# A two-layer hybrid decoder on eight cores: reads tracked apart, diagonals and pooled sums on GpSimd, activations time-major

## The chip, the cores and the metric

One Trainium2 chip, 8 NeuronCores. Every core works on two of the sixteen sequences with the same program; no core talks to another. The metric is the device time of the slowest core in microseconds. In the profile TensorE is PE (its weight loads PEld), VectorE DVE, ScalarE ACT, GpSimd POOL, SyncE SP.

## What is computed

The reference, cut to what the change touches:

```python
# x: (16, 2048, 1024); per layer (2 layers), h = rms_norm(x) @ w_in, split in za, zb, zc
a, gate = split(za); y = a * sigmoid(gate)              # mixer A: 384 channels
y = causal_depthwise_conv(y, width 31) + conv_b
ya = silu(layer_norm(y)) @ w_pw
u, v = split(gelu(zb)); v = layer_norm(v)               # mixer B: 4 heads x 96
yb = u * (tril(w_s) @ v per chunk of 128 + b_s)
yc = ((trailing mean over 2/4/8/16 positions of zc) - zc) @ w_pool * pool_scale   # mixer C
x = x + concat(ya, yb, yc) @ w_out
x = x + (silu(rms_norm(x) @ w_gate) * (rms_norm(x) @ w_up)) @ w_down
# after the last layer: rms_norm(x)
```

## The kernel before

The residual `xT` stays in SBUF in float32, channels on partitions, 2048 positions, in four tiles j of 512. A layer runs so: for each tile norm1 makes `xb` (bf16, not yet divided by the rms) and the factor `r1`; `A` (L626) makes the gated values of the tile, `ytok`, stores them to DRAM (`yd`) and reads them back in another order, `y2`, by eight DMAs of 16 partitions each (L648 on). `toep_closures` (L653) spreads the filter taps into `toep`. `conv` (L667) multiplies `y2` (as the stationary operand) with `toep` and leaves `xc`, 128 blocks on partitions, 384 channels x 16 positions in a block free. `lna_closures` (L682) and `lnt` (L707) do the LayerNorm over channels, per position of the block, and transpose into `silT` with SiLU. `V` (L719) and `U` (L744) project mixer B's halves with Gelu, V's LayerNorm gives `vn`; `SP` (L754) mixes positions, `TR` (L763) transposes. `Zprep` (L774) makes r along the free axis: `split` writes r in three bf16 parts, `dia` multiplies an identity by them into twelve diagonals `dsp`, `bc` multiplies those by ones on TensorE. `Z` (L779) projects mixer C, scales by that broadcast `rbc` into `zc`, and builds the trailing sums by doubling; `PM` (L806) applies `w_pool`. `PW` (L812), `WO` (L821), `norm2` (L833; it uses the same diagonals) and the `FFN` follow. Between two sequences `fin_store` (L598) transposes the result and stores it by way of `osA` (three buffers) and `osB` (two), from the same SyncE queue that carries `yd` and `y2`.

What sets the order: every engine executes its own queue in program order. `P.add` (L89) puts the instruction at the end of its engine's queue and computes its semaphore waits from `Buf` objects: a writer waits for the last writer and all readers of the same `Buf`, and of every `Buf` whose byte range overlaps (`ov`, L80 to L83). A DMA's completion is a semaphore too, so a DMA that writes a `Buf` waits, on the queue that issues it, until the DMA that wrote the `Buf` before has landed. Small work is put into the queues between matmul groups: `push` (L384) appends a closure to `bg` (or to `lo`), each `tick` (L393) executes the first of `bg`, or of `lo` where `bg` is empty, `need(tag)` (L400) executes `bg` until the tag is done, `drain` (L408) executes all. PSUM has eight banks, given out in turn; a matmul waits for the bank's last reader.

`w_a`, `w_uv` come by two DMAs each into one `Buf`; `load_w_rest` (L441) ends with the triangular mask of `wsT`, a GpSimd operation that waits for that DMA. All constants, identity included, share one `Buf`, `bC`. Weights are loaded by GpSimd's queue. The order by hand in the main loop before, tile by tile: V0, U0, conv, Zprep0, SP0, V1, Z0, Zprep1, TR0, U1, PM0, SP1, V2, Z1, ... Z3, TR3, `lnt` 1 to 3, then PW and WO.

## Time and profile before

| what | us |
|---|---|
| median of 3 runs (lowest to highest) | 3668.67 (3633.67 to 3855.72) |
| profiled execution, whole | 3630.46 |
| its span, slowest core (cores 3613.8 to 3628.2) | 3628.2 |
| PE busy / DVE / ACT / POOL over the span | 2787.5 / 1384.3 / 820.5 / 276.7 |
| mean granted TensorE clock (1 is 2.4 GHz, 0.5 is 1.2 GHz) | 0.886 |
| a half of `w_a` or `w_uv` from issue to landing, median | 10.1 / 10.7 |
| one read `y2` from issue to landing, median (48 KB, 512 packets) | 2.2 |
| a store `yd` from issue to landing, median | 2.8 |

The span is what the stages below are cut from; 2.3 us of the execution lie around it. Pieces of the mixer, from the grouped view, mean of one in ns: sum with PSUM `zc` 683, `xc` from PSUM 692, `ybt` 617 (four a tile), `bn_stats` of `vg` 560 and of `xc` 784, each with an aggregate of 182, apply on `xc` 639, pow on GpSimd 1013 to 1024, `pp` 975, the five small ones of `split` 165 each (about 1.35 us with their gaps). A projection of 16 matmuls of 512 columns took 3.62 us at full clock, V's 32 matmuls of 384 columns 5.4 us.

Times are us from the start of the span. In a timeline a row has start, length, engine, line, operation, what it writes and reads, how many are merged, and in brackets the engine's idle time just before and what ended it. A line is mostly that of a helper (L365 `tt`, L371 `ts`, L377 `stt`, L355 `act_op`, L326 `mm`, L318 `dma`), so one goes by the names of tiles.

### The profile page before, as it was taken

The numbers are of one execution on the slowest core, as the hardware profiler recorded it, in microseconds if no ns is written. First come the engines' busy times: TensorE is split into PE (matmuls) and PEld (weight loads), VectorE is DVE, ScalarE is ACT, GpSimd is POOL, SyncE is SP. The second block draws the span as 40 slices with busy tenths as digits, with TensorE's granted clock in tenths as the row PEclk, the third lists the DMA queues.
The fourth block names the chain that finished last, engine by engine and source line by source line (L and its number), as shares of the span: only waits on it lengthen the run. The fifth ranks groups of instructions, "written<-read, shape, count | busy, mean of one in ns | idle before, by whom it ended". The sixth has DMA issues, their size and how long they took to land.

```text
span 3628.2 us, 43607 instructions; the slowest of 8 cores (3613.8 to 3628.2 us)
## 1 busy us (share of the span) xinstructions
PE 2787.5 (77%) x14864; PEld 1387.4 (38%) x14864; DVE 1384.3 (38%) x2657; ACT 820.5 (23%) x1240; POOL 276.7 (8%) x347
## 2 busy tenths in 40 slices
PE   4444879999824679999955448899997346799998
PEld 3332334444422334444443223344444223344444
DVE  2264433323435352233433535233232453432335
ACT  3314210011512421100333242100124124101102
POOL 1012000000011101000000220100000121000000
PEclk9776989999966789999987768899998677899999
DMA  7301232120210305221332030412102003012212
GB/s 152 53 1 20 39 58 53 24 41 12 42 25 1 58 1 81 41 41 30 100 110 43 1 58 2 75 35 41 24 12 50 17 1 58 12 25 52 36 23 93
DMA packets 123847, 148.98 MB, mean 41 GB/s; under 512 B 71664, under 2 KB 98800, under 8 KB 121584
## 3 DMA queue, kind: packets, MB, share of 16 engines
q0 software_dynamic: 36224, 96.61, 15.9%
q1 hardware_dynamic: 87408, 49.59, 4.9%
q8 instruction: 124, 2.03, 0.2%
q14 instruction: 91, 0.75, 0.1%
HBM read 219.71 MB, written 23.07 MB: 67 GB/s over the span
## 4 chain that ended last, share of the span: by engine, by line
PE 65%; DMA 12%; DVE 11%; issue 5%; POOL 4%; ACT 2%; DVEq 1%; SPq 0%; POOLq 0%; ACTq 0%
PE bank L326 62%; DMA y<-yd 8%; DVE dsp L371 3%; DMA yd<-ytok 2%; POOL zF L365 2%; ACT silT L355 1%; PE bank L336 1%; PE bank L344 1%; POOL zG L365 1%; DVE h2T L377 1%; DVE ybt L377 1%; DVE pp L377 1%; DVE vg L377 1%; DVE bnv L730 1%; DMA w_a_sb<-w_a 1%
## 5 line engine op out<-in xcount | busy, mean ns | idle before, releaser
L326 PE MATMUL bank<-h2T,ring 128*128 128x512 bf16 x5632 | 1237.3, 383 | 39.4 <-DVE h2T L377 39.4
L326 PEld LDWEIGHTS bank<-h2T,ring 128*128 128x128 bf16 x5632 | 553.8, 99 | 718.4 <-issue 67.1
L326 PE MATMUL bank<-act,wd 128*128 128x512 bf16 x2816 | 618.1, 379 | 7.5 <-DVE r L371 3.7
L365 DVE TENSOR_TENSOR xT<-xT,bank 128x512 f32<-128x512 f32 x640 | 439.8, 687 | 473.1 <-PE bank L326 394.8
L365 DVE TENSOR_TENSOR act<-tsil,bank 128x512 bf16<-128x512 f32 x352 | 242.0, 688 | 973.7 <-PE bank L326 961.9
L355 ACT ACTIVATE tsil<-bank 128x512 f32<-128x512 f32 x352 | 210.1, 597 | 1588.6 <-PE bank L326 1585.5
L326 PEld LDWEIGHTS bank<-act,wd 128*128 128x128 bf16 x2816 | 269.9, 98 | 323.4 <-issue 8.0
L326 PE MATMUL bank<-dsp,onesb 128*128 128x512 bf16 x96 | 41.1, 558 | 355.3 <-DVE dsp L371 355.3
L355 ACT ACTIVATE sqr<-xT 128x512 bf16<-128x512 f32 x320 | 192.5, 623 | 205.1 <-PE bank L524 194.0
L336 PE MATMUL bank<-toep,y 128*128 128x128 bf16 x576 | 45.0, 253 | 196.1 <-DMA y<-yd 196.1
L326 PE MATMUL bank<-w_uv_sb,xb 128*128 128x384 bf16 x1024 | 193.3, 351 | 0.0
L326 PE MATMUL bank<-w_a_sb,xb 128*128 128x384 bf16 x1024 | 178.8, 331 | 1.7 <-DVE r L371 1.7
L326 PEld LDWEIGHTS bank<-dsp,onesb 128*128 128x128 bf16 x96 | 8.6, 113 | 374.4 <-issue 373.4
L326 PEld LDWEIGHTS bank<-w_uv_sb,xb 128*128 128x128 bf16 x1024 | 107.1, 105 | 83.3 <-issue 27.8
L326 PEld LDWEIGHTS bank<-w_a_sb,xb 128*128 128x128 bf16 x1024 | 97.0, 99 | 63.1 <-issue 6.5
L336 PEld LDWEIGHTS bank<-toep,y 128*128 128x128 bf16 x576 | 44.6, 157 | 197.5 <-issue 197.5
L371 DVE TENSOR_SCALAR dsp<-identb,spb 128x128 bf16<-128x128 bf16 x384 | 97.4, 254 | 42.2 <-DVE dsp L371 3.0
L326 PE MATMUL bank<-ya,wo 128*128 128x512 bf16 x384 | 112.9, 406 | 0.0
L326 PE MATMUL bank<-ybT,wo 128*128 128x512 bf16 x384 | 108.6, 393 | 0.0
L355 ACT ACTIVATE silT<-bank,pv 128x512 bf16<-128x512 f32 x48 | 107.6, 2655 | 0.1
L318 POOL DMA_DIRECT2D ring<-w_gate_up x88 | 47.1, 539 | 739.9 <-PE bank L326 715.2
L344 PE MATMUL bank<-identF,xc 128*128 128x128 f32 x192 | 35.7, 351 | 83.4 <-DVE xc L372 80.6
(100 smaller groups left out, 1893.4 us busy)
## 6 DMA issues: line engine op xcount, KB each, us to landing
ring<-w_gate_up POOLq DMA_DIRECT2D x88, 512.0 KB, 7.3
wd<-w_down POOLq DMA_DIRECT2D x12, 1536.0 KB, 11.7
xst<-x SPq DMA_DIRECT2D x32, 512.0 KB, 10.1
out<-osF SPq DMA_DIRECT2D x16, 512.0 KB, 5.0
w_a_sb<-w_a POOLq DMA_DIRECT2D x8, 768.0 KB, 10.1
w_uv_sb<-w_uv POOLq DMA_DIRECT2D x8, 768.0 KB, 10.7
yd<-ytok SPq DMA_DIRECT2D x16, 384.0 KB, 2.8
y<-yd SPq DMA_DIRECT2D x128, 48.0 KB, 2.2
```

Source lines behind the costliest of these rows:

```text
L318: return P.add(q, lambda e, out=out, in_=in_: e.dma_start(out=out, in_=in_), reads=reads, writes=writes, dma=True, final=final)
L326: ins = e.matmul(out, l, r, start=(first and i == 0), stop=(last and i == n - 1))
L336: ins = e.matmul(out, l, r, start=(i == 0), stop=(i == n - 1))
L344: ins = e.transpose(out, in_, idn)
L355: return e.activation(out=out, in_=in_, func=func, **kw)
L365: return P.add(eng, lambda e, out=out, in0=in0, in1=in1, op=op: e.tensor_tensor(out=out, in0=in0, in1=in1, op=op), reads=reads, writes=writes)
L371: return e.tensor_scalar(out=out, in0=in0, scalar1=s1, scalar2=None, op0=op0)
L377: e.scalar_tensor_tensor(out=out, in0=in0, scalar=scalar, in1=in1, op0=op0, op1=op1),
L730: vec(lambda e, q=q: e.bn_stats(out=bnv[:, q * 6:q * 6 + 6], in_=vg[:, q, :]), [vg.b(q, lo=1536 * q, n=1536)], [bst])
```

## The change

`Buf` gets a group: ranges of the same group don't count as overlapping. With it each of the eight reads into `y2`, and each half of `w_a` and `w_uv`, is tracked on its own. The twelve diagonal writes on VectorE become one GpSimd `tensor_tensor` of 128x1536 with both inputs broadcast. In Z both chains of sums are issued on GpSimd, the ScalarE copies of the lower partitions go (tile halves are written directly, or copied on GpSimd), and what reads them on VectorE (`fin`) is queued behind four empty closures each. `silT` is stored time-major, so that ScalarE writes in order; PW reads it with a stride and writes PSUM in order. V's LayerNorm becomes closures; `vn` and `pp` get a second buffer. The constants come before the first weight load and have two `Buf`s, the mask comes after A(3). The order of the main loop is new. The diff, cut to its core (not shown: the buffers' places, `vconv` and `toep` with `bC2`, `w_a.b(0 or 1)` in A's read lists):

```diff
-    def buf(self, *key, rng=None):
+    def buf(self, *key, rng=None, grp=None):
...
                 for o in self.ranged:
+                    if grp is not None and o.grp == grp:
+                        continue
                     if o.rng[0] < rng[1] and rng[0] < o.rng[1]:
...
-        dma("gpsimd", w_a[:, :, DA:2 * DA], w_a_d[l, :, :, DA:2 * DA], [], [w_a.b()])
-        dma("gpsimd", w_a[:, :, 0:DA], w_a_d[l, :, :, 0:DA], [], [w_a.b()])
+        dma("gpsimd", w_a[:, :, DA:2 * DA], w_a_d[l, :, :, DA:2 * DA], [], [w_a.b(1, grp="w_a")])
+        dma("gpsimd", w_a[:, :, 0:DA], w_a_d[l, :, :, 0:DA], [], [w_a.b(0, grp="w_a")])
...
         dma("gpsimd", wsT[:], w_s_d[l], [], [B("wsT")])
+
+    def mask_ws():
         pool(lambda e: e.affine_select(out=wsT[:], in_=wsT[:], pattern=[[0, 4], [1, 128]], compare_op=ALU.is_ge,
                                        fill=0.0, base=0, channel_multiplier=-1), [B("wsT"), bC], [B("wsT")])
...
     x_dma(0, 0)
-    load_w_a(0)
     pool(lambda e: e.memset(identF[:], 1.0), [], [bC])
...
     pool(lambda e: e.memset(ocS[:], 1.0 / 1024.0), [], [bC])
+    load_w_a(0)
+    dma("sync", pv[:], pv_d, [], [bPV])
     x_dma(0, 1)
     x_dma(0, 2)
-    dma("sync", pv[:], pv_d, [], [bPV])
...
-        def dia(i):
-            for q in range(4):
-                ts(dsp[:, i, q, :], identb[:], spb[:, i, q:q + 1], None, ALU.mult, None, [bs, bC], [bd])
+        def dia():
+            tt(dsp[:].rearrange("p i q t -> p (i q) t"), identb[:].unsqueeze(1).to_broadcast([128, 12, 128]),
+               spb[:].rearrange("p i q -> p (i q)").unsqueeze(2).to_broadcast([128, 12, 128]), ALU.mult,
+               [bs, bC], [bd], eng="gpsimd")
...
         push(split)
-        push(lambda: dia(0))
-
-        def dia12():
-            dia(1)
-            dia(2)
-        push(dia12)
+        push(dia)
+        if late is not None:
+            late()
         push(bc, (kind + "bc", s, l, j))
...
-    def y2b(u):
+    def y2b(u, i):
         if u < 0:
             return y2.b("h", n=2 * 2 * NG)
-        return y2.b(u, lo=(2 + 32 * u) * NG * 2, n=32 * NG * 2)
+        return y2.b(u, i, lo=(2 + 32 * u) * NG * 2, n=32 * NG * 2, grp="y2")
...
             dma("sync", y2[TB * i:TB * (i + 1), 2 + 32 * j:2 + 32 * (j + 1), :], src[i, :, 32 * j:32 * (j + 1), :],
-                [byd], [y2b(j)])
+                [byd], [y2b(j, i)])
...
-            mms(groups, [y2b(u) for u in range(-1, NJ)] + [toep_b(b)], [bb])
+            mms(groups, [y2b(-1, 0)] + [y2b(u, i) for u in range(NJ) for i in range(NI)] + [toep_b(b)], [bb])
...
-            dst = silT[:, ct, :].rearrange("p (b t) -> p t b", t=TB)[:, 4 * tq:4 * tq + 4, :]
+            dst = silT[:, ct, 4 * tq:4 * tq + 4, :]
             act_op(dst, bk[:].rearrange("p (t b) -> p t b", t=4), AF.Silu, [bb, bPV],
-                   [silT.b(ct, tq, lo=4096 * ct, n=4096)], scale=pvc(l, PV_LNG + ct), bias=pvc(l, PV_LNB + ct))
+                   [silT.b(ct, tq, lo=4096 * ct + 1024 * tq, n=1024)], scale=pvc(l, PV_LNG + ct), bias=pvc(l, PV_LNB + ct))
...
     def V(s, l, j):
-        rd = [bxb(j, k) for k in range(8)] + [w_uv.b()]
+        def vstat(q):
+            bst = B("bnv")
+            vec(lambda e: e.bn_stats(out=bnv[:, q * 6:q * 6 + 6], in_=vg[:, q, :]),
+                [vg.b(q, lo=1536 * q, n=1536)], [bst])
+            vec(lambda e: e.bn_aggr(out=bnv[:, 24 + 2 * q:26 + 2 * q], in_=bnv[:, q * 6:q * 6 + 6]), [bst], [bst])
...
             tick()
+            push(lambda q=q: vstat(q))
+            tick()
         bst = B("bnv")
-        for q in range(4):
-            vec(lambda e, q=q: e.bn_stats(out=bnv[:, q * 6:q * 6 + 6], in_=vg[:, q, :]),
-                [vg.b(q, lo=1536 * q, n=1536)], [bst])
-        for q in range(4):
-            vec(lambda e, q=q: e.bn_aggr(out=bnv[:, 24 + 2 * q:26 + 2 * q], in_=bnv[:, q * 6:q * 6 + 6]), [bst], [bst])
-        mvv = bnv[:, 24:32].rearrange("p (q t) -> p q t", t=2)
-        ts(bnv[:, 32:36], mvv[:, :, 1], LN_EPS, None, ALU.add, None, [bst], [bst])
-        pool(lambda e: e.tensor_tensor(out=bnv[:, 32:36], in0=bnv[:, 32:36], in1=mhalf[:, 0:4], op=ALU.pow),
-             [bst, bC], [bst])
-        for q in range(4):
+        vn = vn2[j % 2]
+
+        def pw():
+            mvv = bnv[:, 24:32].rearrange("p (q t) -> p q t", t=2)
+            ts(bnv[:, 32:36], mvv[:, :, 1], LN_EPS, None, ALU.add, None, [bst], [bst])
+            pool(lambda e: e.tensor_tensor(out=bnv[:, 32:36], in0=bnv[:, 32:36], in1=mhalf[:, 0:4], op=ALU.pow),
+                 [bst, bC], [bst])
+
+        def ap1(q):
             stt(vg[:, q, :], vg[:, q, :], bnv[:, 24 + 2 * q:25 + 2 * q], sgB[:, 0, :], ALU.subtract, ALU.mult,
                 [vg.b(q, lo=1536 * q, n=1536), bst, sgB.b()], [vg.b(q, lo=1536 * q, n=1536)])
+
+        def ap2(q):
             stt(vn[:, q, :], vg[:, q, :], bnv[:, 32 + q:33 + q], sgB[:, 1, :], ALU.mult, ALU.add,
                 [vg.b(q, lo=1536 * q, n=1536), bst, sgB.b()], [vn.b(q, lo=768 * q, n=768)])
+        push(pw)
+        for q in range(4):
+            push(lambda q=q: ap1(q))
+        for q in range(4):
+            push(lambda q=q: ap2(q), ("vn", s, l, j) if q == 3 else None)
...
-            tick()
+            tick(2)
 
     def SP(s, l, j):
+        need(("vn", s, l, j))
+        vn = vn2[j % 2]
         for h in range(4):
...
-            tick()
...
+    def Zprep(s, l, j, late=None):
         def sink(bk, bb):
             act_op(rbc[:], bk[:], AF.Copy, [bb], [rbc.b()])
-        split_bcast_closures(s, l, j, r1, "r1", sink)
+        split_bcast_closures(s, l, j, r1, "r1", sink, late)
...
             tt(zc[:, m, ZH:ZH + NT], bk[:], rbc[:], ALU.mult, [bb, rbc.b()], [zc.b()])
-            tick()
+            tick(2)
         W = ZH + NT
+        z0, z1 = zc[:, 0, :], zc[:, 1, :]
+
+        def pt(out, i0, i1, rd, wr):
+            tt(out, i0, i1, ALU.add, rd, wr, eng="gpsimd")
+
+        def m0():
+            pt(zG[:, 1:W], z0[:, 1:W], z0[:, 0:W - 1], [zc.b()], [zG.b()])
+            pt(zF0[64:128, :], zG[64:128, ZH:W], zG[64:128, ZH - 2:W - 2], [zG.b()], [zF0.b()])
+            pt(zF0[0:64, :], z0[0:64, ZH:W], z0[0:64, ZH - 1:W - 1], [zc.b()], [zF0.b()])
+
+        def m1():
+            pt(zG[:, 1:W], z1[:, 1:W], z1[:, 0:W - 1], [zc.b(), zF0.b()], [zG.b()])
+            pt(zF[:, 3:W], zG[:, 3:W], zG[:, 1:W - 2], [zG.b()], [zF.b()])
+            pt(zG[:, 7:W], zF[:, 7:W], zF[:, 3:W - 4], [zF.b()], [zG.b()])
+            pt(zF[64:128, ZH:W], zG[64:128, ZH:W], zG[64:128, ZH - 8:W - 8], [zG.b()], [zF.b()])
+            pool(lambda e: e.tensor_copy(out=zF[0:64, ZH:W], in_=zG[0:64, ZH:W]), [zG.b()], [zF.b()])
+
+        def fin(m):
+            f = zF0[:, :] if m == 0 else zF[:, ZH:W]
+            fb = zF0.b() if m == 0 else zF.b()
+            zm = zc[:, m, :]
+            out, ob = (pp0, B("pp0")) if m == 0 else (pp1, pp1.b())
+            stt(out[:], f, invw[:, m:m + 1], zm[:, ZH:W], ALU.mult, ALU.subtract, [fb, zc.b(), bC2], [ob])
+            if j == 0:
+                tt(f[:, 0:ZH], f[:, 0:ZH], invcnt[:, m, :], ALU.mult, [fb, bC2], [fb])
+                tt(out[:, 0:ZH], f[:, 0:ZH], zm[:, ZH:2 * ZH], ALU.subtract, [fb, zc.b()], [ob])
+        m0()
+        m1()
+        for i in range(4):
+            push(lambda: None)
+        push(lambda: fin(0))
+        for i in range(4):
+            push(lambda: None)
+        push(lambda: fin(1), ("pp", s, l, j))
+
+    def PM(s, l, j):
+        need(("pp", s, l, j))
         for m in range(2):
-            zm = zc[:, m, :]
-            tt(zG[:, 1:W], zm[:, 1:W], zm[:, 0:W - 1], ALU.add, [zc.b()], [zG.b()], eng="gpsimd")
-            tt(zF[:, 3:W], zG[:, 3:W], zG[:, 1:W - 2], ALU.add, [zG.b()], [zF.b()], eng="gpsimd")
-            if m == 1:
-                tt(zG[:, 7:W], zF[:, 7:W], zF[:, 3:W - 4], ALU.add, [zF.b()], [zG.b()], eng="gpsimd")
-                tt(zF[:, 15:W], zG[:, 15:W], zG[:, 7:W - 8], ALU.add, [zG.b()], [zF.b()], eng="gpsimd")
-            act_op(zF[0:64, ZH:W], zG[0:64, ZH:W], AF.Copy, [zG.b()], [zF.b()])
-            stt(pp[:, m, :], zF[:, ZH:W], invw[:, m:m + 1], zm[:, ZH:W], ALU.mult, ALU.subtract,
-                [zF.b(), zc.b(), bC], [pp.b()])
-            if j == 0:
-                tt(zF[:, ZH:2 * ZH], zF[:, ZH:2 * ZH], invcnt[:, m, :], ALU.mult, [zF.b(), bC], [zF.b()])
-                tt(pp[:, m, 0:ZH], zF[:, ZH:2 * ZH], zm[:, ZH:2 * ZH], ALU.subtract, [zF.b(), zc.b()], [pp.b()])
-
-    def PM(s, l, j):
-        for m in range(2):
-            bk, bb = next_bank()
-            mm(bk[:], [(wpl[:, m, :], pp[:, m, :])], [pp.b(), B("wpl")], [bb])
+            bk, bb = next_bank()
+            mm(bk[:], [(wpl[:, m, :], (pp0 if m == 0 else pp1)[:])], [B("pp0") if m == 0 else pp1.b(), B("wpl")], [bb])
             act_op(yc[j][:, m, :], bk[:], AF.Identity, [bb, bPV], [yc[j].b()], scale=pvc(l, PV_PS + m))
 
     def PW(s, l, j):
         y = ya[j % 2]
         for co in range(3):
             bk, bb = next_bank()
-            mm(bk[:], [(w_pw[:, ci, co * 128:(co + 1) * 128], silT[:, ci, jc(j)]) for ci in range(3)],
-               [silT.b(ci, tq, lo=4096 * ci, n=4096) for ci in range(3) for tq in range(4)] + [B("w_pw")], [bb])
+            mm(bk[:].rearrange("p (b t) -> p b t", t=TB),
+               [(w_pw[:, ci, co * 128:(co + 1) * 128],
+                 silT[:, ci, :, 32 * j:32 * (j + 1)].rearrange("p t b -> p b t")) for ci in range(3)],
+               [silT.b(ci, tq, lo=4096 * ci + 1024 * tq, n=1024) for ci in range(3) for tq in range(4)] + [B("w_pw")], [bb])
...
             drain()
+            mask_ws()
+            V(s, l, 0)
+            U(s, l, 0)
             load_wo(l, 0)
             load_wo(l, 1)
-            V(s, l, 0)
-            U(s, l, 0)
-            conv()
+
+            def cv():
+                while bg:
+                    pop(bg)
+                conv()
+            Zprep(s, l, 0, cv)
             lna_closures(s, l)
-            Zprep(s, l, 0)
-            SP(s, l, 0)
-            V(s, l, 1)
-            Z(s, l, 0)
-            Zprep(s, l, 1)
-            TR(s, l, 0)
-            U(s, l, 1)
-            PM(s, l, 0)
-            SP(s, l, 1)
...
-            PM(s, l, 2)
-            SP(s, l, 3)
-            lnt(s, l, 0)
-            Z(s, l, 3)
-            load_wo(l, 2)
-            TR(s, l, 3)
-            lnt(s, l, 1)
-            lnt(s, l, 2)
-            lnt(s, l, 3)
+            for j in range(NJ):
+                Z(s, l, j)
+                if j + 1 < NJ:
+                    Zprep(s, l, j + 1)
+                    need(("vn", s, l, j))
+                    V(s, l, j + 1)
+                SP(s, l, j)
+                TR(s, l, j)
+                if j + 1 < NJ:
+                    U(s, l, j + 1)
+                else:
+                    for tq in range(4):
+                        lnt(s, l, tq)
+                    load_wo(l, 2)
+                PM(s, l, j)
             for fp in range(NRING):
                 load_ring(l, fp, fp)
             PW(s, l, 0)
-            PM(s, l, 3)
             load_wd(l, 0)
             PW(s, l, 1)
```

## Rows read from the trace of the kernel before

**Rows 1.** Waits over the span: engine line, waited for, us in total, times, longest.

```profile
PE bank L326 <- DVE dsp L371: 355.3, 32, 23.0
...
PE bank L336 <- DMA y<-yd: 196.1, 4, 56.4
...
PE bank L344 <- DVE xc L372: 80.6, 8, 15.3
...
PE bank L344 <- DVE osB L377: 35.9, 2, 18.2
```

**Rows 2.** Timeline of SyncE's DMA queue, and a window: busy by engine, PEclk, DMA share, GB/s.

```profile
1021.36 0.38 SPq L318 DMA_DIRECT2D yd<-ytok  x1
...
1026.32 16.64 SPq L318 DMA_DIRECT2D y<-yd  x8
...
1000.00:1016.00 16.00, 0.00 (x0) 0.00 (x0) 0.00 (x0) 0.00 (x0) 0.00 (x0) 0.50 0.17 21
```

**Rows 3.** Timeline before conv, second layer, TensorE and ScalarE.

```profile
978.27 10.56 PE L326 MATMUL bank<-w_uv_sb,xb 128*128 128x384 bf16 x64
...
990.03 0.93 ACT L355 ACTIVATE toep<-vconv,M 128x768 bf16<-128x768 bf16 x1 [0.62 <-DVE toep L371]
...
1045.27 11.06 PE L336 MATMUL bank<-toep,y 128*128 128x128 bf16 x144 [56.43 <-DMA y<-yd]
```

**Rows 4.** Windows behind it: conv to zc of tile 0, three cycles, LayerNorm tail.

```profile
1045.27:1078.07 32.80, 26.12 (x227) 18.78 (x227) 24.36 (x55) 2.92 (x5) 1.08 (x2) 0.89 0.01 1
...
1078.07:1195.88 117.81, 51.61 (x279) 28.34 (x279) 59.92 (x149) 33.24 (x48) 25.95 (x23) 0.71 0.00 1
...
1195.88:1227.31 31.43, 5.59 (x24) 4.88 (x25) 9.92 (x19) 22.71 (x13) 11.53 (x14) 0.50 0.29 47
```

**Rows 5.** Timeline of one tile cycle, GpSimd, VectorE and TensorE.

```profile
1120.10 1.06 POOL L365 TENSOR_TENSOR zG<-zc 128x527 f32<-128x527 f32 x1 [7.18 <-DVE zc L365]
...
1123.30 1.57 POOL L365 TENSOR_TENSOR zG<-zc 128x527 f32<-128x527 f32 x1 [0.93 <-ACT zF L355]
...
1127.47 1.26 POOL L365 TENSOR_TENSOR zF<-zG 128x513 f32<-128x513 f32 x1
...
1129.63 0.75 DVE L377 SCALAR_TENSOR_TENSOR pp<-zF,invw,zc 128x512 bf16<-128x512 f32 x1 [5.68 <-ACT zF L355]
...
1131.85 4.23 DVE L371 TENSOR_SCALAR dsp<-identb,spb 128x128 bf16<-128x128 bf16 x12
...
1136.33 1.44 PE L326 MATMUL bank<-dsp,onesb 128*128 128x512 bf16 x3 [22.10 <-DVE dsp L371]
```

**Rows 6.** Grouped by form: xcount, busy us, mean ns, then idle before.

```profile
L377 DVE SCALAR_TENSOR_TENSOR vn<-vg,bnv,sgB 128x384 bf16<-128x384 f32 x64 | 39.5, 618 | 6.7
...
L730 DVE BATCH_NORM_STATS2 bnv<-vg 128x6 f32<-128x384 f32 x64 | 35.9, 560 | 129.4 <-ACT vg L355 124.4
...
L448 POOL TENSOR_SCALAR_AFFINE_SELECT wsT<-wsT 128x512 bf16<-128x512 bf16 x4 | 2.5, 634 | 51.1 <-DMA wsT<-w_s 51.1
```

**Rows 7.** Grouped by form: ScalarE's SiLU outputs, TensorE's weight loads.

```profile
L355 ACT ACTIVATE silT<-bank,pv 128x512 bf16<-128x512 f32 x48 | 107.6, 2655 | 0.1
...
L355 ACT ACTIVATE tsil<-bank 128x512 f32<-128x512 f32 x352 | 210.1, 597 | 1588.6 <-PE bank L326 1585.5 <-DVE h2T L377 3.2
...
L336 PEld LDWEIGHTS bank<-toep,y 128*128 128x128 bf16 x576 | 44.6, 157 | 197.5 <-issue 197.5
...
L326 PEld LDWEIGHTS bank<-silT,w_pw_sb 128*128 128x128 bf16 x144 | 15.1, 107 | 57.6 <-issue 44.7
```

**Rows 8.** Timeline of the start, GpSimd and TensorE.

```profile
26.51 0.88 POOL L318 DMA_DIRECT2D w_a_sb<-w_a  x1 [23.87 <-DMA w_a_sb<-w_a]
...
33.58 0.66 PE L344 MATMUL bank<-identF,xst 128*128 128x128 f32 x2 [33.58 <-DVE invcnt L498]
...
65.30 0.63 POOL L448 TENSOR_SCALAR_AFFINE_SELECT wsT<-wsT 128x512 bf16<-128x512 bf16 x1 [19.75 <-DMA wsT<-w_s]
...
66.45 1.07 POOL L538 TENSOR_TENSOR r<-r,mhalf 128x4 f32<-128x4 f32 x1
```

71 lines of the change are left out of this document (33 added, 38 removed).

## The prediction, made before the kernel was run

> **What bounds the kernel now.** I read the profile in this order: the sum of waits over the whole run, the stages of one layer, then that layer's queues in order of time. No engine is the bound over the run. In the waits [rows 1] the reader is to see four pauses of TensorE that all lie inside the token mixer: 355.3 us for `dsp` (the diagonals that broadcast r), 196.1 us for the reshuffled `y2`, 80.6 us for the normalised `xc`, 35.9 us for `osB`. Together 668 us of 3628. The FFN, where TensorE is dense, isn't touched by the change. So I work out the mixer of the second layer and carry it to all four (two sequences, two layers).
>
> First, the convolution's input. SyncE sends the eight reads of a tile one behind another: 16.64 us for eight [rows 2], because all eight write one `Buf` (`y2b(j)`), and each waits until the one before has landed, though they fill other partitions. While that goes on the DMA engines are 0.17 busy [rows 2]. TensorE ends U(0) at 978.27 + 10.56 = 988.8, and starts conv at 1045.27, 56.4 later [rows 3]; the mean over four layers is 196.1/4 = 49.0 [rows 1]. Second, the stages behind it [rows 4]: conv to the second `zc` of tile 0 32.8 us, three tile cycles 117.8 (39.3 each, granted clock 0.71), the LayerNorm tail up to PW(0) 31.4. VectorE is busy 59.9 of the 117.8, so it is order and latency, not load, that sets a cycle. Rows 5 show how: GpSimd builds the pooled sums from 1120.10 to 1128.7, with a trip to ScalarE in each half; VectorE stands in its queue at `pp` until 1129.63, and `split` and the twelve `dsp` writes (4.23 us) are behind it, so that TensorE, which had all else done, waits 22.10 us.
>
> **The change, part by part** (second layer, then times four).
>
> *Reads tracked apart.* In the new order the last `yd` store leaves at about 979.4, right after the last `ytok`. From its issue to the first read that waits for it took 1026.32 less 1021.36, 5 us, in a busy moment [rows 2]; I take 4. Eight reads are issued in about 3 us (the issue of a DMA on SyncE took 0.3 to 0.4), and the last lands about 2.2 later: near 989. DMA capacity: 0.17 of sixteen engines for 16 us is 2.7 us of all sixteen, which fits. The next thing that is late is ScalarE: its last `toep` ends at 990.03 + 0.93 = 991.0 [rows 3], then come a table load of 1.3 and the first Gelu, which frees the first PSUM bank at about 993. So 56.4 becomes about 4, and over the run 196.1 - 4 x 4 = 180 us go. Behind it VectorE has V(0)'s LayerNorm (four statistics, pow, eight applies: 3.8 + 1.7 + 5.0 from 992.8, with the split 1004.6) and then twelve conv evictions at 0.65, to 1012.4; rbc lies over `cbB`, so it waits for the last of them; second `zc` about 1016.5. From conv start 23.5 us against 32.8 [rows 4]: -9 a layer.
>
> *Tile cycle.* New path from one second `zc` to the next: eight GpSimd operations at a pitch of 1.2 for the long ones (1.06 and a hop, [rows 5]), 9.3; `fin(1)` 0.75 + 0.3; split 1.35; diagonals on GpSimd; broadcast 1.2 + 0.2; U's last three products 3.9 at 2.4 GHz or 6.5 in part at 1.2, 5.2 taken; PM 0.5; Z 3.6; `zc` 0.9. V (5.4 us) now lies beside the GpSimd chain, and the two ScalarE copies are gone. The diagonals aren't in the trace as a GpSimd operation. 128x527 took 1.06 us [rows 5], 2.0 ns an element, so 1536 elements are 3.1 us; bounds: the one-input 128x512 at 0.634 [rows 6], three times, 1.9; the slow 1.57 of the same sum [rows 5], scaled, 4.6. I take 3.1 + 0.2, because the form is the same. Sum 26.6, say 27, against 39.3: -37 a layer for three cycles. VectorE's load in such a cycle is about 16 us (eight applies at 0.62 [rows 6], statistics 3.5, `ybt` 2.8, the rest 4.5), so it doesn't become the bound; GpSimd has 9.3 + 3.3 + 1.0.
>
> The slow 1.57 started while VectorE's `pp` ran [rows 5], 0.5 more than its neighbours. By the Trainium skill, "SBUF — State Buffer", section "Who interferes with whom", a VectorE instruction with two SBUF inputs and a GpSimd instruction that reads SBUF exclude each other; by that rule the applies and `ybt` may each push the GpSimd chain or be pushed, and the trace agrees as far as this one row goes. It speaks against moving diagonals to GpSimd. The sum goes by the unslowed row; if every second GpSimd operation were slowed by 0.5 it would be 2.3 more a cycle, 27 us over the run.
>
> *LayerNorm work.* Ticks: a cycle has 24 slots (Z 4, V 8, TR 4, U 8), and its `bg` queue now gets 26 entries (eight empty, two `fin`, three of Zprep, four statistics, pw, eight applies), so `lo`, which holds conv's LayerNorm, is served only by the four ticks of Z(0). Nearly all of it falls behind Z(3): `ts` and pow wait behind the GpSimd chain (10.7 after `zc`), applies and `fin` to 13.9, then three groups of 3.9 statistics + 1.5 pow + 2.3 applies (and one 0.7), to 37.7, transposes 2.8, activation 0.6. Tail about 41.5 against 31.4 [rows 4]: +10 a layer. In that tail the SiLU output before cost 2655 ns each, its write being strided, where a like operation with a plain write costs 597 [rows 7]; the 2 us saved each are hidden now behind VectorE, except the last ones, which the 41.5 holds.
>
> *The price of time-major.* PW now reads its moving operand with 256 bytes between neighbours. 36 matmuls a layer. No moving read like it is in the trace. Lower bound zero: the matmul could hide it. Nearest row: TensorE's own strided read, `y2` as weights, 157 ns against 107 for `w_pw` [rows 7], about a doubling of the streaming part; the far one is the strided write of ScalarE, 2655/597 = 4.4 times. Taking a doubling, 0.22 on 512 columns: +8 a layer; at 4.4 times, 0.73 each, +26 a layer. By the Trainium skill, "SBUF — State Buffer", in the note on cachelines under "Door 1: The DMA port swizzle (why `[64,N]` ≈ `[32,N]`)", each access that crosses to a new 16-byte line pays a penalty. The trace agrees for weights and for ScalarE's writes; for the moving side no row here shows it.
>
> *Start.* GpSimd waits for the first half of `w_a` before it makes the constants (26.51), TensorE starts at 33.58, and `r` stands on GpSimd behind the `wsT` mask until 65.30 [rows 8]. Now the constants come first, halves don't wait for each other, the mask comes after A(3). The second half of `w_a` should land near 37 (26.5 plus the 10.1 that such a half takes, page, part 6), where TensorE now resumes at 68.9: -30, bounds -20 (it lands at 47) and -35.
>
> *Second sequence.* Its `osB` stores stand on SyncE behind eight reads. 35.9 us in two waits [rows 1]; store and landing remain, 4 each: -28.
>
> *Costed at nothing:* norm2's diagonals on GpSimd (3.3 against 4.23 on VectorE, [rows 5], four a layer). GpSimd's earlier ring and `wd` loads wait for the tail and PM(3), which end before. If they didn't, each such wait would show before a broadcast.
>
> Sum: four times (-45 - 9 - 37 + 10 + 8) = -292, -30, -28: -350. Against the profiled execution 3628 - 350 = 3278, with 2.3 us around the span 3280. The median of the runs is 38 above the profiled one, the lowest 3 above; I forecast 3290.
>
> **Rivals.**
> 1. *The strided read costs as much as the strided write.* +26 instead of +8 a layer: 3362. For: both kinds of strided access in the trace are slow. Against: TensorE's own is only 1.5 times.
> 2. *The cycle doesn't shorten.* The broadcast ends up behind GpSimd, whose queue takes pooled sums, pow and diagonals in turn, or the `fin` slots come too late: 39.3 stays, +148, 3438. Against: the slots before `fin(1)` are over when V and SP are.
> 3. *Parallel reads aren't parallel.* If eight still took 17 us, 180 and 28 stay: 3498. Against: 0.17 DMA share.
> 4. *Slower than before.* One mechanism: the 256-byte stride on the moving side. It has to eat 350 + 32 = 382 us over 144 matmuls, 2.65 each, so it decides from 3.0 us a matmul. ScalarE's strided write took 2.655 for 512 elements, which still leaves 3628 - 382 + 327 = 3573. Only beyond that is it slower, say 3650.
> 5. *More is gained*: moving read free, low clock gone: 3220.
>
> **How the numbers follow.** Forecast (3220 to 3345) 0.66; rival 1 0.13; rival 2 0.09; rival 3 0.03; rival 4 0.02; rival 5 (below 3220) 0.07. The range 3215 to 3390 takes the forecast and rival 1 whole and a little of 2 and 5: about 0.82. About 2% is what a measurement of this kernel tells from no change. Slower by over 2% 0.02, within 2% (3595 to 3742) 0.02, all else 0.96.
>
> **What would show it.** In the profile after: TensorE's wait for `y` under 10 us a layer, the eight reads issued within 3 us; `dsp` a GpSimd operation of about 3.1 us; distance between second `zc`s about 27; wait for `xc` grown to some 30 us a layer; `silT` near 0.6; the PW matmul at 0.6 rather than 0.38; TensorE's first transpose well before 30. Wrong would be: a PW matmul over 1 us, GpSimd late at every broadcast, or the reads still 2 us apart.

## The result and the profile after

Measured beside the kernel before: 0.932 of its time, 95% interval 0.921 to 0.943; profiled execution 3401.28 us (before 3630.46), median of 4 runs 3457.65 (3397.40 to 3720.51) against 3655.48 of the kernel before, run in turn with it. In two of the four executions a whole die ran slower, which lifts the median; the ratios here and below leave such executions out. Faster by 6.8% where 9.4% had been forecast (3290 of 3630), and outside the range on its slow side. Cores that do the same work ended 55 us apart, and pairs of them (0 and 1, 2 and 3, 6 and 7) had a lower granted clock, 0.81, for a while, the longest stretches lying in the FFN. So core 5, which had none of that, shows what the kernel does, and core 0, the last to end, sets the time.

The cores of after, span and mean granted clock:

```profile
core 0: 3399.7 us, clock 0.892
...
core 5: 3344.8 us, clock 0.914
```

The stages, cut by the same marks in every kernel; "zc 2" is the start of the second `zc` of a tile, "tail" below is the stretch from there in tile 3 to PW(0). Four values are the four passes (two sequences, two layers); before is its slowest core, 3628.2.

| stage | before | after, core 5 | sum of the four | forecast |
|---|---|---|---|---|
| V(0) begins for the first time | 121.6 | 88.8 | -33 | -30 |
| V(0) to conv | 57.4, 67.0, 47.4, 66.5 | 15.7, 17.3, 16.9, 17.3 | -171 | -180 |
| conv to zc 2 of tile 0 | 31.7, 32.1, 32.4, 32.2 | 20.7, 19.1, 19.6, 19.1 | -50 | -36 |
| three tile cycles, each | 39.18, 39.27, 38.67, 39.51 | 27.05, 26.45, 27.02, 26.46 | -149 | -148 |
| zc 2 of tile 3 to PW(0) | 32.2, 32.1, 32.1, 32.1 | 42.4, 42.3, 42.2, 42.3 | +41 | +40 |
| PW(0) to the first `down` product | 196.2, 196.3, 198.9, 196.1 | 222.4, 222.4, 222.5, 222.4 | +102 | +32 |
| first `down` product of pass 2 to V(0) of pass 3 (second sequence, A part) | 504.4 | 481.3 | -23 | -28 |

Together -283, the difference of the two spans. All rows but one came out within 14 us of their forecast. The rows that follow are of core 0, up to the strided product. The waits over the span (engine line, waited for, us in total, times, longest), to be held against [rows 1]:

```profile
PE bank L331 <- POOL dsp L370: 110.1, 28, 6.0
...
PE bank L349 <- DVE xc L377: 78.2, 16, 5.6
```

`dsp` waits fell from 355.3 to 110.1, but not all of these 245 us were won: TensorE now waits 59.5 us for `ybt` and 25.0 for `vn`, which the list of before doesn't have. `y` and its 196.1 are gone from the list, and the reads of the last tile are issued in 4.14 us where they took 16.64 [rows 2]. SyncE's DMA queue, last `yd` and the reads behind it:

```profile
921.47 0.38 SPq L323 DMA_DIRECT2D yd<-ytok  x1
926.81 4.14 SPq L323 DMA_DIRECT2D y<-yd  x8
```

One tile cycle of after, GpSimd and TensorE, for [rows 5]:

```profile
955.94 1.06 POOL L370 TENSOR_TENSOR zG<-zc 128x527 f32<-128x527 f32 x1 [8.65 <-DVE zc L370]
...
964.86 0.60 POOL L831 COPY zF<-zG 64x512 f32<-64x512 f32 x1
965.37 1.44 PE L349 MATMUL bank<-identb,ybt 128*128 128x128 bf16 x12 [7.00 <-DVE ybt L382]
968.23 2.75 POOL L370 TENSOR_TENSOR dsp<-identb,spb 128x1536 bf16<-128x1536 bf16 x1 [2.78 <-DVE spb L575]
...
971.23 1.18 PE L331 MATMUL bank<-dsp,onesb 128*128 128x512 bf16 x3 [2.42 <-POOL dsp L370]
```

The whole chain of sums stays on GpSimd, from 955.94 to 965.46; the diagonals are one operation of 2.75; TensorE waits 2.42 for them, not 22.10, and 7.00 for `ybt` ahead of that. The windows that answer to [rows 4] (conv to zc 2, three cycles, tail; cut, as there, at the end of the `zc`):

```profile
935.96:955.73 19.77, 18.88 (x184) 15.21 (x185) 16.50 (x36) 2.29 (x5) 4.91 (x5) 0.88 0.51 82
955.73:1036.63 80.90, 56.67 (x284) 28.80 (x281) 48.27 (x96) 23.62 (x41) 37.81 (x30) 0.81 0.00 1
1036.63:1078.15 41.52, 14.67 (x66) 11.72 (x67) 29.17 (x54) 12.15 (x16) 14.04 (x14) 0.59 0.08 13
```

The row that missed is the one with the strided product. By form, before and then after:

```profile
L326 PE MATMUL bank<-silT,w_pw_sb 128*128 128x512 bf16 x144 | 39.4, 426 | 35.8 <-ACT silT L355 35.8
...
L331 PE MATMUL bank<-silT,w_pw_sb 128*128 128x512 bf16 x144 | 125.7, 1036 | 1.7 <-ACT silT L360 1.7
...
L360 ACT ACTIVATE silT<-bank,pv 128x512 bf16<-128x512 f32 x48 | 36.3, 776 | 64.5 <-PE bank L349 63.1
```

Overlapping matmuls inflate the mean; merged runs give the pitch (a run also holds the drain of its last product, so 9 come out 0.01 to 0.02 us dearer each than 18). Second layer, core 5 of after: 18 in 15.63 us, then twice 9 in 7.89, 0.87 each. Before, 9 took 2.11 at full clock, 0.23 each; the first nine of its pass took 3.54, most of it at a granted 0.50. First before, then after:

```profile
1231.12 2.11 PE L326 MATMUL bank<-silT,w_pw_sb 128*128 128x512 bf16 x9
...
1050.81 15.63 PE L331 MATMUL bank<-silT,w_pw_sb 128*128 128x512 bf16 x18 [0.42 <-ACT silT L360]
...
1082.14 7.89 PE L331 MATMUL bank<-silT,w_pw_sb 128*128 128x512 bf16 x9
```

The `silT` output on ScalarE fell from 2655 ns [rows 7] to 776; those 90 us of ScalarE lay mostly behind VectorE in the new tail; e2 finds that they bought 4.7 us a pass.

### The profile page after: what moved, and what is told of

Same layout as the page of the kernel before. It is cut to its first block, busy times and chain, and to the rows that moved or that the text cites. A ratio compares the mean times of both kernels' runs of the same rounds, so it can differ in the third digit from the quotient of the medians.

```text
span 3399.7 us, 43152 instructions; the slowest of 8 cores (3344.8 to 3399.7 us)
## 1 busy us (share of the span) xinstructions
PE 2990.8 (88%) x14864; PEld 1428.0 (42%) x14864; DVE 1312.5 (39%) x2273; ACT 736.4 (22%) x1208; POOL 395.7 (12%) x411
## 4 chain that ended last, share of the span: by engine, by line
PE 78%; DVE 7%; POOL 7%; issue 3%; DMA 2%; ACT 2%; SPq 0%; DVEq 0%; POOLq 0%; ACTq 0%
PE bank L331 75%; POOL dsp L370 2%; POOL zF L370 2%; PE bank L349 1%; POOL zG L370 1%; DVE bna L696 1%; DVE xc L377 1%; DMA w_a_sb<-w_a 1%; DVE h2T L382 1%; PE bank L532 1%; ACT toep L360 1%; PE bank L341 1%; DVE vn L382 1%; DVE zc L370 0%; POOL bna L701 0%
## 5 line engine op out<-in xcount | busy, mean ns | idle before, releaser
L331 PE MATMUL bank<-h2T,ring 128*128 128x512 bf16 x5632 | 1269.6, 390 | 31.5 <-DVE h2T L382 31.5
L331 PE MATMUL bank<-act,wd 128*128 128x512 bf16 x2816 | 630.8, 384 | 7.5 <-DVE rF L376 3.7
L331 PE MATMUL bank<-w_uv_sb,xb 128*128 128x384 bf16 x1024 | 210.4, 372 | 0.0
L323 POOL DMA_DIRECT2D ring<-w_gate_up x88 | 46.9, 537 | 839.1 <-PE bank L331 838.7
L331 PE MATMUL bank<-dsp,onesb 128*128 128x512 bf16 x96 | 41.9, 568 | 110.1 <-POOL dsp L370 110.1
L546 POOL TENSOR_TENSOR r<-r,mhalf 128x4 f32<-128x4 f32 x32 | 32.6, 1020 | 859.4 <-DVE r L376 840.5
L331 PE MATMUL bank<-silT,w_pw_sb 128*128 128x512 bf16 x144 | 125.7, 1036 | 1.7 <-ACT silT L360 1.7
L331 PE MATMUL bank<-ya,wo 128*128 128x512 bf16 x384 | 124.3, 439 | 0.0
L331 PE MATMUL bank<-ybT,wo 128*128 128x512 bf16 x384 | 118.1, 421 | 0.0
L349 PE MATMUL bank<-identF,xc 128*128 128x128 f32 x192 | 44.7, 421 | 78.2 <-DVE xc L377 78.2
L532 PEld LDWEIGHTS bank<-ocS,sqr 128*128 128x128 bf16 x1280 | 70.3, 98 | 68.5 <-issue 30.8
L370 POOL TENSOR_TENSOR dsp<-identb,spb 128x1536 bf16<-128x1536 bf16 x32 | 87.9, 2748 | 77.2 <-DVE spb L575 64.6
L382 DVE SCALAR_TENSOR_TENSOR h2T<-xT,pv,bank 128x512 bf16<-128x512 f32 x128 | 88.2, 741 | 18.8 <-PE bank L331 18.8
```

Of the source, the lines that this page charges most:

```text
L323: return P.add(q, lambda e, out=out, in_=in_: e.dma_start(out=out, in_=in_), reads=reads, writes=writes, dma=True, final=final)
L331: ins = e.matmul(out, l, r, start=(first and i == 0), stop=(last and i == n - 1))
L349: ins = e.transpose(out, in_, idn)
L370: return P.add(eng, lambda e, out=out, in0=in0, in1=in1, op=op: e.tensor_tensor(out=out, in0=in0, in1=in1, op=op), reads=reads, writes=writes)
L382: e.scalar_tensor_tensor(out=out, in0=in0, scalar=scalar, in1=in1, op0=op0, op1=op1),
L532: ins = e.matmul(bk[:, q:q + 1], sqr[i][:, q * 128:(q + 1) * 128], ocS[:, 0:1], start=(k == 0 and q == 0), stop=(k == 7), skip_group_check ...
```

## The experiments

Four questions: is the 102 us the stride of the moving operand; what does a stride cost; how much of the forecast's sum belongs to the reads; and what are the 55 us between core 0 and core 5. Where a kernel has a core without the granted 0.81, called undisturbed here, the times are taken on it. e3, e4, e7, e10 and e13 were executed once each.

### e1: PW reads `silT` in order

```diff
-            mm(bk[:].rearrange("p (b t) -> p b t", t=TB),
+            mm(bk[:].rearrange("p (t b) -> p t b", t=TB),
                [(w_pw[:, ci, co * 128:(co + 1) * 128],
-                 silT[:, ci, :, 32 * j:32 * (j + 1)].rearrange("p t b -> p b t")) for ci in range(3)],
+                 silT[:, ci, :, 32 * j:32 * (j + 1)]) for ci in range(3)],
-            act_op(y[:, co, :], bk[:], AF.Copy, [bb], [y.b()])
+            act_op(y[:, co, :].rearrange("p (b t) -> p b t", t=TB), bk[:].rearrange("p (t b) -> p b t", t=TB), AF.Copy,
+                   [bb], [y.b()])
```

> The changed kernel with one thing different: PW reads silT in the order it lies in (runs of 32 neighbours, 64 bytes), its result stays time-major in PSUM, and ScalarE's copy into ya reorders it while reading PSUM. Theory A (the missing time is the 256-byte stride of PW's moving operand): 18 PW matmuls took 15.63 us, 0.87 each, against 2.11 for 9 (0.23 each) in the kernel before, so 36 x 0.64 = 23 us a layer go, and with them the low granted clock behind PW (3 us a layer): about 100 us of the whole, 3400 becomes 3300 on the slowest core. Theory B (the WO part is longer because the denser mixer draws the clock down, and the PW matmuls merely stretch with it): the matmuls stay over 0.5 us, and the stretch from PW(0) to the FFN stays over 145 us. Theory C (the granted 0.81 in the first 120 us of the FFN comes from the slow PW matmuls ahead of it): the FFN stretch of the first sequence goes from 440 back to 419 on all cores; if it comes from the dense mixer, 0.81 stays.

Measured: 3325.03 profiled, median 3314.85 (before, run in turn with it, 3635.14), where 3300 was expected. PW(0) to the first `down` product is 191.9 us on core 3 in its first pass, against 222.4; in the other passes, and on core 1 in all four, about 211.6. The matmul is back at a mean of 379 ns, so theory A's price of the stride holds and B falls. The reordering moved into ScalarE's read of PSUM and costs nothing there: `ya` 595 ns, 597 in after, where it was plain. Grouped by form, core 1:

```profile
L331 PE MATMUL bank<-silT,w_pw_sb 128*128 128x512 bf16 x144 | 33.0, 379 | 1.7 <-ACT silT L360 1.7
L360 ACT ACTIVATE ya<-bank 128x512 bf16<-128x512 f32 x48 | 28.2, 595 | 122.5 <-PE bank L331 120.0 <-ACT ya L360 0.4
```

The 20 us that come back in those passes are a clock, not work. Core 1, windows in the FFN (us, PE, PEld, DVE, ACT, POOL busy, granted clock, DMA share, GB/s):

```profile
380.00:390.00 10.00, 5.33 (x13) 1.95 (x14) 4.53 (x7) 0.60 (x1) 0.00 (x0) 0.50 0.01 2
390.00:400.00 10.00, 10.00 (x39) 4.13 (x38) 1.75 (x3) 1.20 (x2) 4.75 (x7) 0.81 0.53 77
...
530.00:540.00 10.00, 10.00 (x48) 4.54 (x47) 2.06 (x3) 1.77 (x3) 1.06 (x2) 1.00 0.54 81
```

After half-busy work at 0.50 TensorE is granted 0.81, where core 3 was granted 1.00 in its first pass: 39 products in 10 us, later 48. 0.50 and 1.00 are its two levels, 1.2 and 2.4 GHz; 0.81 is neither, and shows also in windows of 5 us. So the stride is one cause, and the 0.81 a second one. It is there without the slow products, so they aren't what brings it about (theory C). Whether the shorter mixer does was the question for running the same kernel again.

### e12: the same kernel again, at another time and on another chip

No edit against e1.

> e1 once more, word for word. In e1, e2 and the changed kernel most cores took 45 to 105 us more than the least disturbed one, in pairs of cores, with a granted clock of 0.81 at the head of the first two FFNs; e3, e4, e6, e8, e9 and the kernel before hardly show it. Theory D (it belongs to this order of work): the profile shows 0.81 stretches again, and more than half of the core executions are 45 us and more above the lowest. Rival E (it was the chip's state at that hour): it is gone, all cores at about 3225.

Measured: 3235.32 profiled, ratio 0.889 (0.887 to 0.891). All cores end between 3223.4 and 3233.7, PW(0) to `down` is 191.8 to 193.1 everywhere, and no core shows 0.81. Core 5 where e1 had its 0.81:

```profile
390.00:400.00 10.00, 10.00 (x48) 4.56 (x47) 2.07 (x3) 1.79 (x3) 5.56 (x8) 1.00 1.01 134
400.00:500.00 100.00, 100.00 (x465) 45.30 (x463) 33.58 (x49) 10.15 (x17) 2.64 (x5) 1.00 0.53 75
```

The same instructions with and without it: the kernel alone doesn't set off the 0.81. It isn't the chip alone either: e6, e8 and e9 below ran later on the chip of e1 and have none in their profiled executions. But the kernel may still matter, alone or together with the chip and the hour: of the profiled executions after has it on six cores, e1 on eight, e2 on six, e3 and e7 on two each, while before, e4 and the seven others have it on none. So what sets it off stays open. Without it the 30.5 us a pass can be laid out. Windows from PW(0) on, second layer, core 5 of after, then core 5 of this kernel:

```profile
1050.81:1066.50 15.69, 15.69 (x19) 2.31 (x20) 0.00 (x0) 4.11 (x7) 3.29 (x7) 0.58 1.00 181
1066.50:1140.00 73.50, 64.11 (x262) 23.00 (x261) 21.98 (x42) 14.41 (x25) 7.54 (x4) 0.83 0.17 26
1140.00:1195.00 55.00, 47.37 (x242) 20.72 (x240) 22.08 (x38) 11.41 (x20) 3.76 (x2) 0.89 0.00 1
```

```profile
1023.48:1027.50 4.02, 4.02 (x19) 1.84 (x20) 0.00 (x0) 3.65 (x7) 3.29 (x7) 1.00 0.80 103
1027.50:1082.00 54.50, 47.56 (x262) 21.20 (x259) 21.81 (x42) 14.42 (x26) 4.97 (x4) 0.94 0.52 80
1082.00:1137.00 55.00, 44.84 (x242) 20.28 (x242) 22.18 (x39) 11.22 (x20) 6.33 (x3) 0.94 0.00 1
```

The first 18 products cost 11.7 more, the next stretch of 262 products 19.0 more, of which its own 18 strided ones are 11.6 (18 x 0.64). The rest, 7.4, goes with the granted clock (0.83 against 0.94). The clock fell while the slow products ran, and they kept their pace: on core 5 of after, second pass, they begin 0.86 apart in a stretch at 1.00 and 0.86 apart in the one at 0.50 behind it.

```profile
1051.00:1053.00 2.00, 2.00 (x3) 0.23 (x2) 0.00 (x0) 0.93 (x2) 2.00 (x5) 1.00 0.71 78
...
1055.00:1066.40 11.40, 11.40 (x15) 1.73 (x14) 0.00 (x0) 2.39 (x4) 0.00 (x0) 0.50 1.06 199
```

The plain products of e12 in the same place ran at 1.00 throughout.

### e2: `silT` block-major again, everything else as changed

```diff
-    silT = AT("silT", 98304, [128, 3, TB, NBLK], BF16)
+    silT = AT("silT", 98304, [128, 3, S], BF16)
```

and the write strided, the read plain, as before.

> The changed kernel with silT block-major as in the kernel before: ScalarE writes it with a 32-byte stride, PW reads in order. Theory A: PW back to 0.23 us a matmul, -23 -3 us a layer; ScalarE's SiLU back to 2.65 us each, of which only the last group of three is not hidden behind VectorE's LayerNorm: +5 us a layer. Net -21 a layer, -84: time-major as it was done loses more than it brings. Rival: the strided SiLU is on the path in all four groups (+6 each): net about 0.

Measured: 3350.70 profiled, median 3349.79, cores from 3246.2 to 3349.1 (four of them with long stretches at 0.81, two with shorter ones). On core 1 the tail is 46.9 (+4.7), PW(0) to `down` 194.1, `silT` on ScalarE 2642 ns. So the change's time-major output by itself lost: it took 4.7 off a tail and put 28.3 on the stage behind it, some 94 us over the run (84 expected). The undisturbed core, 3246.2 against 3344.8, says the same.

### e7: what a stride costs

PW(0) to PW(3) in the four passes take their moving operand at chosen distances, e.g.

```diff
+        n = (("c", 2, 4), ("x", 8, 16), ("c", 32, 64), (3, "r", 128))[k][max(j - 1, 0)]
+        if 512 * n <= 2048:
+            return f[:, 0:512 * n:n], None
```

(`"c"` in order, `"x"` as changed, `"r"` runs of 32 neighbours, a number the distance in elements of 2 bytes).

> A measurement, not a candidate: PW's moving operand is read with another distance between neighbours in each layer (the output is then another one than the reference's): PW(0) and PW(1) in order / as changed, 256 bytes / in order / 6 bytes; PW(2) 4, 16, 64 bytes and runs of 32; PW(3) 8, 32, 128 and 256 bytes, in the order of the four layers. Theory A1 (each new 16-byte line costs): the time per matmul grows in steps from 0.23 to 0.87 us as fewer of the eight values of a line are used: 2, 4, 8 bytes near 0.23, 16 bytes and beyond 0.87. Theory A2 (any distance but the natural one costs the same): 4 bytes is 0.87 already. Theory A3 (the cost is that of a large power of two): only 128 and 256 bytes are slow.

Measured, merged runs (18 for PW(0) and PW(1), 9 each for the others), core 7, passes 1, 2 and 4, in the order of the list above:

```profile
249.38 4.05 PE L331 MATMUL bank<-silT,w_pw_sb 128*128 128x512 bf16 x18 [0.53 <-ACT silT L360]
267.08 2.20 PE L331 MATMUL bank<-silT,w_pw_sb 128*128 128x512 bf16 x9
292.30 4.23 PE L331 MATMUL bank<-silT,w_pw_sb 128*128 128x512 bf16 x9
...
1048.05 15.63 PE L331 MATMUL bank<-silT,w_pw_sb 128*128 128x512 bf16 x18 [0.45 <-ACT silT L360]
1079.36 8.26 PE L331 MATMUL bank<-silT,w_pw_sb 128*128 128x512 bf16 x9
1111.86 8.42 PE L331 MATMUL bank<-silT,w_pw_sb 128*128 128x512 bf16 x9
...
2703.28 6.28 PE L331 MATMUL bank<-silT,w_pw_sb 128*128 128x512 bf16 x18 [0.34 <-ACT silT L360]
2723.21 2.11 PE L331 MATMUL bank<-silT,w_pw_sb 128*128 128x512 bf16 x9
2747.23 7.88 PE L331 MATMUL bank<-silT,w_pw_sb 128*128 128x512 bf16 x9
```

| bytes between neighbours | 2 | 4 | 6 | 8 | 16 | 32 | 64 to 256 | runs of 32, then a jump |
|---|---|---|---|---|---|---|---|---|
| us of one matmul of 512 columns | 0.225 | 0.24 | 0.35 | 0.47 | 0.92 | 0.94 | 0.87 | 0.23 |

Theory A3 falls, 16 bytes being as slow as 256, and A2, 4 bytes being nearly free. A1 is right from 16 bytes on and wrong at 8, for which it foretold 0.23. What fits all values is a count: how many values of a row lie in one piece of 16 bytes. Four or more are free or nearly so, 2.7 cost 1.5 times, two twice, one four times, and from there on the distance hardly matters. Why it is so no run shows. The longest times don't depend on the granted clock, as the rows under e12 show: 0.86 apart at 1.00 and at 0.50. So with a new piece for every column a column takes about 1.7 ns, and the price of a 256-byte stride is 0.64 a matmul, not the 0.22 of the forecast.

### e3 and e8: the reads one behind another

```diff
-        return y2.b(u, i, lo=(2 + 32 * u) * NG * 2, n=32 * NG * 2, grp="y2")
+        return y2.b(u, lo=(2 + 32 * u) * NG * 2, n=32 * NG * 2)
```

> The changed kernel with the eight reads into y2 tracked by one Buf per tile again, all else kept. The forecast's step says: TensorE's wait before conv comes back to 49 less the 8 to 9 us that are there now (+40 a layer, +160), and the two osB waits (+28): 3590. Rival: the rest of the new order (GpSimd, VectorE filled with V(0)'s LayerNorm during the wait) makes use of that wait, and only +25 a layer, +100, comes back.

Measured: 3567.86, core 0 3534.0; V(0) to conv 63.1, 62.8, 44.3, 65.9 and conv to zc 2 17.0. On undisturbed cores, core 0 against core 5 of after, that is 3534.0 - 3344.8 = 189 (160 + 28 expected, the rival's 100 falls): the parallel reads are two thirds of what the whole change won there.

The same edit on e1 (e8):

> e1 with the eight reads tracked by one Buf again. Two questions. First, additivity: an undisturbed core of e1 took 3222, e3 less after gave 190 (3534 against 3345), so 3412 on an undisturbed core. Second, the granted 0.81 ahead of the FFN's first products: if it comes from the mixer being dense (theory C1), it is rarer here than in e1 (there 20 of 32 core executions were held back by 45 us and more), as it was in e3; if it comes from the order of the work behind conv (theory C2), it is as frequent as in e1.

Measured: 3434.13, ratio 0.943 (0.942 to 0.945); V(0) to conv 64.9, 64.3, 44.6, 60.8 on core 2, the first to end (3405.2). Against 3223.4, the first of e12, that is 182, and last against last, 3432.3 against 3233.7, 199. So the reads are worth about the same with and without the stride: the two parts add up. None of its cores shows 0.81; as e12 doesn't either, that decides nothing between C1 and C2.

### e4 and e13: the kernel before with the reads alone

Only the tracking (`grp`, `y2b(u, i)`) is put into the kernel before.

> The kernel before with one part of the change: the eight reads tracked apart. V(0) to conv falls from 57.4, 67.0, 47.4, 66.5 to 17 each (-170), the two osB waits give 23. V(0)'s LayerNorm, hidden in the wait before, now lies ahead of conv's evictions on VectorE: +3 a layer. Together -181: 3628 becomes 3447. Rival (reads in parallel are only worth their full time together with the new order): less than -120.

Measured: 3482.95, 147 won where 181 was expected, span 3481.4. V(0) to conv 27.1, 26.8, 24.1, 26.2, not 17; conv to zc 2 32.2; the wait for `dsp` 353.7, untouched. SyncE's queue, core 5, shows the 10 us that are missing:

```profile
952.26 0.46 SPq L321 DMA_DIRECT2D yd<-ytok  x1
968.03 4.45 SPq L321 DMA_DIRECT2D y<-yd  x8
```

15.8 us from the store to the first read, in after 5.34; over the four passes 13.2 to 18.0. The eight reads are as quick as there (4.45); it is the store that lands late. In this kernel two `wo` loads are issued just ahead of V(0). They are so in the kernel before too, but there the last store stands behind the reads of the other tiles and leaves 24 to 43 us after V(0) begins (2 to 5 here), and the first read follows it by 5.0 to 5.6.

Those two loads moved behind U(0) (e13):

```diff
-            load_wo(l, 0)
-            load_wo(l, 1)
             V(s, l, 0)
             U(s, l, 0)
+            load_wo(l, 0)
+            load_wo(l, 1)
             conv()
```

> e4 with the two first loads of wo after U(0), as the change has them. In e4 V(0) to conv was 24 to 27 us instead of the 17 of the changed kernel, and the last yd store took 15.8 us from issue to the first read that waits for it (968.03 less 952.26), where it took 5.3 in the changed kernel. Theory: that is wo's transfer on the same DMA engines; with the loads later V(0) to conv is 17, -35 over the run against e4, 3446. Rival: it is the order of VectorE and ScalarE; V(0) to conv stays at 26.

Measured: 3462.74, where 3446 was expected. On core 5 store to read is back at 4.2 us, 4.2 to 6.6 over the four passes:

```profile
942.88 0.38 SPq L321 DMA_DIRECT2D yd<-ytok  x1
947.06 4.49 SPq L321 DMA_DIRECT2D y<-yd  x8
```

V(0) to conv is 19.3, 17.7, 17.0, 17.8, but conv to zc 2 rises from 32.2, 32.0, 33.3, 32.0 to 33.3, 35.4, 35.9, 34.7. Conv starts 7 to 9 us earlier, and 1 to 3.4 are given back behind it, where TensorE then waits for VectorE (4.62 for `dsp` before the broadcast of tile 0, at 980.55): -20 in all between the slowest cores. In after both stages are short, about 17 and 19.6. So the gain of the reads hangs on which loads were issued just ahead of the store; how much the rest of the change adds behind conv wasn't taken apart further. In both kernels PW(0) to `down` is some 2 us longer than before (about 198.5 for 196.8 in the mean over all cores), which stays unexplained.

### e6, e9, e11, e10: LayerNorm pieces in slots of the cycle

In after `lo` isn't served in the cycles. Two ways of serving it, both on top of e1. First (e6), the empty closures carry one piece each:

```diff
+        def slot():
+            if lo:
+                pop(lo)
         for i in range(4):
-            push(lambda: None)
+            push(slot)
```

(the same for the second four).

> e1 with one thing different: the eight empty closures around fin(0) and fin(1) of each tile execute one piece of conv's LayerNorm each. Theory A (VectorE has room in a cycle, the LayerNorm tail of 42.3 us is there only because the queue lo gets no slots): all but eight pieces are done by Z(3), the tail falls to about 17 us, and each cycle grows by 2 to 3 us, because the pieces stand ahead of fin(1), split and so the diagonals: 27 becomes 29.5. Net -17 a layer, -68. Rival (a cycle is bound by VectorE once the work is in it): the cycle grows by the full 6.5 us, +20 a layer against -25: no gain.

Measured: 3264.10, ratio 0.897 (0.896 to 0.899). The tail falls from 42.3 to 21.6 (17 expected), a cycle rises from 27 to between 34.9 and 35.7 on core 0 (2 to 3 more expected, 6.5 by the rival): three times 8 lost, 21 won, and 3 more lost between PW(0) and `down`. It is 29 us slower than e12, the same kernel without the pieces. VectorE in a cycle, core 0:

```profile
923.07 1.68 DVE L377 TENSOR_SCALAR xc<-xc,bna 128x384 f32<-128x384 f32 x3 [8.29 <-POOL bna L701]
```

GpSimd at the same time:

```profile
912.43 1.06 POOL L370 TENSOR_TENSOR zG<-zc 128x527 f32<-128x527 f32 x1 [8.48 <-DVE zc L370]
...
921.92 1.04 POOL L701 TENSOR_TENSOR bna<-bna,mhalf 128x4 f32<-128x4 f32 x1
```

The apply waits 8.29 us for a pow that stands on GpSimd behind the pooled sums, and V's LayerNorm waits on VectorE behind the apply. A piece of work for an in-order engine is dear when it needs another engine's busy queue.

Second (e9), two pieces behind each U product, and the slots only in the last tile:

```diff
             tick(2)
+            for _ in range(2):
+                if lo:
+                    pop(lo)
...
+        def slot():
+            if j == NJ - 1 and lo:
+                pop(lo)
```

> As e6, but the LayerNorm pieces are executed two after each of U's products, behind the diagonals, where VectorE waits for the next zc; the empty closures serve only in the last tile. Theory A: the cycle grows by 0 to 1.5 us, the tail falls to 17: -21 a layer against e1, -85. Rival: VectorE is still behind when zc comes, the cycle grows by 3 or more, and e9 is no better than e6.

Measured: 3172.09 profiled, **ratio 0.872 (0.870 to 0.874)**, the fastest version of the study, ahead of both kernels and 63 us below e12. Cycle 26.8 to 27.9, tail 21.5 where 17 was expected. Windows of core 4, second pass: three cycles, and the tail to 3 us into PW:

```profile
888.50:971.00 82.50, 56.46 (x284) 29.91 (x285) 64.87 (x128) 24.15 (x41) 41.63 (x33) 0.81 0.00 1
971.00:995.00 24.00, 13.35 (x72) 10.24 (x74) 13.82 (x22) 12.89 (x18) 14.75 (x17) 0.72 0.28 46
```

VectorE does 64.87 us of work in a time in which it did 48.27 in after, and the cycle is about 0.5 longer. Against e12 a pass wins 20.8 in the tail and loses 2 in the three cycles and 3.3 between PW(0) and `down`, where the first 18 products of PW now run at a mean granted 0.72 instead of 1.00. So the 10 us a pass that the change put on the tail, and some 5 more, were avoidable.

With the 256-byte stride put back into e9 (the first diff reversed, e11):

> e9 with PW reading at 256 bytes as in the changed kernel. By stages: PW to the first down product back from 195.6 to 222.4 and somewhat more, +27 a layer, 3168 becomes 3277. That would give the price of the stride a second time, on another kernel. For the granted 0.81: if the long idle tail ahead of PW is what sets it off (theory D1), it stays away here; if the slow PW does, it comes.

Measured: 3284.24, ratio 0.904 (0.900 to 0.907); PW(0) to `down` 222.9 to 223.1 against 195.5 to 195.9 on the slowest cores, +27.3 a pass, span +112. No core shows 0.81, though the slow products are back. This is the price of the stride without the 0.81, with what the stride itself does to the clock.

e9 with the diagonals back on VectorE, twelve operations (e10):

```diff
-            tt(dsp[:].rearrange("p i q t -> p (i q) t"), ..., ALU.mult, [bs, bC], [bd], eng="gpsimd")
+            for i in range(3):
+                for q in range(4):
+                    ts(dsp[:, i, q, :], identb[:], spb[:, i, q:q + 1], None, ALU.mult, None, [bs, bC], [bd])
```

> e9 with the diagonals back on VectorE, twelve operations. The forecast's step says: 4.23 us on VectorE against 2.75 and two hops, about 3.1, on GpSimd: +1.2 a cycle, and as much for each norm2 that TensorE waits for, 12 x 1.2 + 4 x 3 = +26. Rival (the gain of the move is that VectorE is free for other work): with the LayerNorm pieces in the same queue the cycle grows by the full 4.2, +50 and more. Second rival: GpSimd's share was late anyway, nothing changes.

Measured: 3243.92, 72 more than e9: a cycle 30.3 (+2.8), conv to zc 2 +2 to +5, PW(0) to `down` 200.5 (+5). Expected were 26 by the forecast's step, 50 and more by the rival; the total is the rival's, the cycle lies between (1.2 and 4.2). Grouped by form, this kernel and e9:

```profile
L376 DVE TENSOR_SCALAR dsp<-identb,spb 128x128 bf16<-128x128 bf16 x384 | 97.8, 255 | 42.6 <-DVE dsp L376 3.0
```

```profile
L370 POOL TENSOR_TENSOR dsp<-identb,spb 128x1536 bf16<-128x1536 bf16 x32 | 87.9, 2748 | 76.9 <-DVE spb L575 76.9
```

97.8 us of work against 87.9: GpSimd is hardly quicker at it. Of the 72, 34 are in the twelve cycles (12 x 2.8). Two parts can be read in the second cycle of the second pass. With its gaps the work ends 4.45 us behind the split on VectorE (956.70 to 961.15), 2.96 on GpSimd (929.62 to 932.58). From there to the next `zc` it is 10.5 against 9.0: the LayerNorm pieces on VectorE are pushed back, and `zc` follows them without a pause, where in e9 VectorE stood ready and waited 0.50 for TensorE. This kernel, then e9:

```profile
971.66 0.69 DVE L370 TENSOR_TENSOR zc<-bank,rbc 128x512 f32<-128x512 f32 x1
...
941.55 0.69 DVE L370 TENSOR_TENSOR zc<-bank,rbc 128x512 f32<-128x512 f32 x1 [0.50 <-PE bank L331]
```

So the move pays because it frees a queue that is full here. In after, whose cycles hold no LayerNorm pieces, its worth wasn't measured.

## Why the forecast was off

By its own steps:

- **Reads apart.** Right: 16 to 17 us from V(0) to conv, reads in 4.14 us (3 foretold), 5.34 from the store to the first read (4 foretold). With the stage behind it -221 against -216, but that close a sum is luck: the first stage fell 9 short of its -180 and the second went 14 beyond its -36. E3 and e8 give 189 and 182 for the reads alone.
- **Tile cycle.** Right: 26.5 to 27.1 for 27; `dsp` 2748 ns for 3.1 us, the sums 9.5 us for 9.3. Rival 2 fell.
- **LayerNorm pushed behind Z(3).** Right: 42.3 for 41.5, and e6 and e9 show that it was `lo` left unserved. But the wait for `xc` on TensorE didn't grow to 30 a layer; it is 78.2 / 4 = 19.6 (in the second layer 3.60, 5.48, 5.63 and 4.80 before the four groups of transposes), as 5.61 for `vn` and 2.18 for `ybt` of the last tile lie in the tail as waits of their own.
- **Start, second sequence.** Right: -33 for -30, -23 for -28.
- **The price of time-major. This step failed.** It took the nearest row, TensorE's strided weights (157 ns against 107), as the measure of a moving operand and came to 0.22 a matmul, +8 a layer. E7 measures 0.64 a matmul; 36 of them are 23.1, and e11 finds 27.3 a pass, the difference going with the lower granted clock during and behind the slow products. Against before it is +25.5. That is rival 1's size (+26), which was given 0.13; its own count was 0.73 a matmul and nothing for the clock, so that the sums agree so well is in part luck. One of the signs that the forecast had named for being wrong came too, a PW matmul over 1 us: the mean is 1036 ns, overlap included, where 0.6 was foretold. What pointed to it was the row that the forecast named as the far end: ScalarE's strided write, 4.4 times (2655 against 597), the same layout at one value per 16 bytes. The stationary row couldn't say much: the weights have 128 columns, and their stride (48 values, 96 bytes) costs 50 ns in 107, 0.4 ns a column, where the moving side pays 1.3 ns more (0.64 / 512).
- **Not in the sum at all: a granted clock of 0.81** in the FFN of the slowest cores. It is 55 us between core 0 and core 5; of these 1.8 are there at the first V(0), 13.6 and 17.2 lie between PW(0) and `down` of the first two passes (236.0 and 239.6 for 222.4), 8.9 and 7.1 in the stretches from `down` to the next V(0) behind them, and the last 6 or so in the mixer. Before had no such stretch, and all its cores lay within 15 us. The forecast had no term for it and weighed none.

The forecast with the two terms as measured: 3278 + 102 - 32 + 55 = 3403; the other rows miss by +9, -14 and less and come to -3 together, which makes the 3400 of core 0's span. With either of the two alone the time would have been inside the range (3348 and 3333). The stride is the kernel's own, shown by e1, e2, e7, e11 and e12. The 0.81 is there in one execution of a kernel and not in another of the same kernel on another chip (e1, e12); whether quicker kernels are more prone to it stays open.

The forecast also weighed that a two-input VectorE instruction and a GpSimd one that reads SBUF exclude each other. In after the `vn` applies lie beside the pooled sums (core 0):

```profile
1036.54 4.57 DVE L382 SCALAR_TENSOR_TENSOR vn<-vg,bnv,sgB 128x384 bf16<-128x384 f32 x4
```

1.14 each, 1054 ns in the mean over 64, where they took 618 [rows 6]. By the Trainium skill, "SBUF — State Buffer", section "Who interferes with whom", such a pair takes turns; the trace agrees. It costs 1.7 us a tile on VectorE (4 x 0.44). What it costs the cycle wasn't isolated; the cycle is as long as forecast without it.

## What to carry over

Before a tile's layout is turned so that one engine writes it plainly, count how many values of each reader's row lie in one 16-byte piece: a moving operand with one per piece made the matmul four times as long, and the reordering was free in ScalarE's read of PSUM behind it. Work taken off an in-order engine pays when work on the path stands behind it in that engine's queue, even if the new engine is hardly quicker (e10). Where queued work is only postponed, the tail gets it back; it is best put where the engine idles and its operands are ready (e9), not into any slot (e6).

## What the runs showed of the hardware

- TensorE's moving operand, bf16: 512 columns take 0.225 to 0.24 us with four or more values per 16 bytes, 0.35 at 6 bytes' distance, 0.47 at 8, and 0.87 to 0.94 from 16 to 256 bytes (e7); at 256 bytes the same at a granted 1.00 and 0.50 (after).
- The granted clock fell from 1.00 to 0.50 during back-to-back strided products (after, core 5), TensorE being marked busy all the while, and rose again behind them; with plain products in their place (e12) it stayed at 1.00.
- ScalarE, 512 values: bf16 written one value per 32 bytes 2639 to 2655 ns (e2, before), PSUM read in reordered form 595 (e1), plain 597 (after).
- GpSimd: product of two broadcast bf16 operands, 128x1536, 2748 ns, 1.8 ns an element.
- A store's way to the first dependent read took 13.2 to 18.0 us when two weight loads were issued just ahead of it (e4), 4.2 to 6.6 when they came later (e13).
- Pairs of cores at a granted 0.81, in stretches of up to 124 us, the longest at the head of a dense FFN (after), 91 to 93 there in e1; none in e12, the same kernel as e1 on another chip.
